# Short requests on GpSimd, another order of the head norms, zero products in waits, and a first feed-forward with rests

## The chip, the core and the metric

The kernel runs on one core of a Trainium2 chip. The core has TensorE (matrix products into PSUM), VectorE, ScalarE and GpSimd (elementwise work), SyncE (it issues most transfers), and 16 DMA engines that all issuing engines share. The metric is the device time of one execution in microseconds, lower being better. The engines run their own lists of instructions side by side and wait for each other through semaphores, so the order within a list is fixed by the program.

## The reference

Two transformer layers are applied to 256 tokens of width 1024, all in float32. Cut to what matters:

```python
# first block
sh1, sc1, gt1, sh2, sc2, gt2 = modulation(c, w_mod, b_mod)      # silu(c) @ w_mod + b_mod, for c and for c_ctx
hx = rms_norm(x, norm1_g) * (1 + sc1) + sh1                     # hc: the same of ctx
ax = latent_attention(qx, k_all, v_all)                         # q, k normalised by head, k_all: ctx and x
convx = short_conv(bx, cx, ux, conv_w)
x = x + gt1 * merge_out(ax, convx, attn_out_g, conv_out_g, w_out)  # norm by head of 64, then w_out
x = x + gt2 * hier_moe(hx2, w_group, w_router, w_gate, w_up, w_down)  # best group of 4, top 2 of its 8 experts
x = rms_norm(x, final_g)
# second block
ada = silu(c_2) @ w_ada + b_ada                                 # nine vectors of 1024
x = x + 0.5 * g1 * ((silu(h @ w_gate_half) * (h @ w_up_half)) @ w_out)   # ffn1, D_FF = 2816
x = x + g2 * ((sigmoid(gate_a) * mla(h) + sigmoid(gate_b) * chunk_attention(h, rel_bias)) @ w_out)
x = x + 0.5 * g3 * (ffn2, as ffn1)
return rmsnorm(x, final_norm)
```

## The kernel before, in words

Activations lie transposed, features on the 128 partitions in eight chunks (KD = 8) and the 256 tokens in the free dimension. Weights come by 2 MB tiles into a ring of six slots of one arena. Nothing is scheduled by a planner: each engine's program is written out by hand.

Most small and middle products are jobs (list `JOBS`). Job j writes PSUM bank j % 4. TensorE opens and closes it (`open_job`, `close_job`, semaphore `job_ready`), VectorE takes the result and frees the bank (`empty_job`, `job_emptied`). Both engines walk the list in one order, so a job that moves, moves on both.

**Head.** ScalarE issues the constants and the rows of gains and biases (`rows_a`, `rows_b`, turned to columns by TensorE), then the positions, the two router matrices and four blocks of the relative bias (L650 to L657). SyncE issues x, ctx and then the ring (L378). ScalarE computes SiLU of the conditions and the squares of x and ctx. TensorE multiplies the condition with w_mod as it arrives, four pieces `mod0` to `mod3` (L993). In TensorE's order the spreading of the token norms (L1013) and `bias_turn` (L1019) stand between mod1 and mod2. VectorE copies `bias_turn` (L1564), computes the angles of the rotary tables from the positions (L1570 to L1584), and only then copies the mod rows (L1594), from which the first norm's gain and shift come. The first large product is `z_k` (a call of `product`, L918), on the normalised ctx and w_kv.

**End of the first attention.** The last two of the eight attention steps put values after turned probabilities (L1114, L1126). The norms of the merged vector need the sum of squares in each head. `head_sums` (L1076) makes them by products of two columns, ScalarE takes the root (L754), VectorE the reciprocal (L1681), TensorE spreads it over the partitions (L1143), VectorE scales (L1687). `late_turn` brings the late part of the modulation into columns (L1002), and the four merge jobs follow.

**Router.** A norm (L934, L698, L1511, L1517, L711), the logits (L918 on `router`), h turned back to rows (L1163), some 6 us of short VectorE instructions that choose experts, the places of tokens (L918 on `route`), clearing of four banks with zeros (L1175), and `gather_pair` (L1183). Then the expert loop: 32 experts, two weight buffers, each with gate and up (L1217) and down (L1236).

**Feed-forward.** The hidden width 2816 is taken in 22 steps of 128. For gate and up both sides are split in a rounded high part and a rest, both of type fp32r, and three products are summed (L1291): ScalarE rounds (L818), VectorE subtracts (L1853). Steps 3 to 22 run in a loop of five turns with four steps each. ffn2 does the same for down (ScalarE L824 and L836, VectorE L1860 and L1899, three groups of eight products). ffn1 multiplies down in plain float32 (eight products in 16 passes). In ffn1 VectorE has beside it two items of w_ada per turn: eight multiply-adds each (L1474, L1477, `mod_item`), summed over partitions by four column products (`ada_columns`, L1323) and taken at L1923.

## Time and profile before

| | |
|---|---|
| median of 3 runs | 1641.79 us (1640.38 to 1643.27) |
| profiled execution | 1641.19 us, span 1639.4 us |
| mean granted clock of TensorE | 0.969 of 2.4 GHz |
| busy in the span | PE 1531.0, PEld 1072.7, DVE 519.7, ACT 331.5, POOL 23.7 us |
| chain that ended last | PE 71%, DMA 21%, DVE 4%, ACT's queue 2% |

PE is TensorE's products, PEld its weight loads, DVE VectorE, ACT ScalarE, POOL GpSimd. A letter q behind a name means the engine's queue, where it issues transfers. The busy time of TensorE is nearly the whole span, but a busy TensorE is not one at its peak, and a stage is read by what it waits for. The granted clock is 1.00 (2.4 GHz) or 0.50 (1.2 GHz) at any moment; values between are means over a stretch.

### The profile page before, as it was taken

The numbers are of one execution on the slowest core, as the hardware profiler recorded it, in microseconds if no ns is written. First come the engines' busy times: TensorE is split into PE (matmuls) and PEld (weight loads), VectorE is DVE, ScalarE is ACT, GpSimd is POOL, SyncE is SP. The second block draws the span as 40 slices with busy tenths as digits, with TensorE's granted clock in tenths as the row PEclk, the third lists the DMA queues.
The fourth block names the chain that finished last, engine by engine and source line by source line (L and its number), as shares of the span: only waits on it lengthen the run. The fifth ranks groups of instructions, "written<-read, shape, count | busy, mean of one in ns | idle before, by whom it ended". The sixth has DMA issues, their size and how long they took to land.

```text
span 1639.4 us, 22374 instructions
## 1 busy us (share of the span) xinstructions
PE 1531.0 (93%) x9594; PEld 1072.7 (65%) x9598; DVE 519.7 (32%) x926; ACT 331.5 (20%) x535; POOL 23.7 (1%) x31
## 2 busy tenths in 40 slices
PE   3899989999999999999999789999899989899996
PEld 1685864444444444434444479999787767799996
DVE  2446241111111111000111165555444362455553
ACT  1213231111111101111111132222110040343441
POOL 0003000000000000000000000000100000000000
PEclk8999879999999999999999989999999999999998
DMA  9648829999999999999999958878585222155540
GB/s 365 254 155 295 305 119 381 426 429 429 431 425 430 429 433 428 429 430 429 426 430 431 350 205 287 277 258 279 176 316 186 97 109 88 67 162 197 179 154 26
DMA packets 115290, 480.35 MB, mean 293 GB/s; under 512 B 6316, under 2 KB 53673, under 8 KB 95793
## 3 DMA queue, kind: packets, MB, share of 16 engines
q1 hardware_dynamic: 111680, 476.99, 74.0%
q10 hardware_dynamic: 3121, 1.18, 0.3%
q0 software_dynamic: 448, 1.59, 0.3%
q8 instruction: 31, 0.51, 0.1%
q14 instruction: 10, 0.08, 0.0%
HBM read 478.68 MB, written 1.06 MB: 293 GB/s over the span
## 4 chain that ended last, share of the span: by engine, by line
PE 71%; DMA 21%; DVE 4%; ACTq 2%; ACT 1%; issue 1%; DVEq 0%
DMA arena<-in_w_up_dram 21%; PE psum L918 17%; PE psum L1291 16%; PE psum L1217 12%; PE psum L1312 8%; PE psum L1236 5%; PE psum L1201 2%; PE psum L1183 2%; PE psum L934 1%; ACTq L657 1%; PE psum L1047 1%; PE psum L1097 1%; PE psum L1126 1%; PE psum L1114 1%; DVE rstd L1511 1%
## 5 line engine op out<-in xcount | busy, mean ns | idle before, releaser
L1217 PE MATMUL psum<-arena,squares 128*64 128x384 f32 x2048 | 341.4, 491 | 20.0 <-DMA arena<-in_w_up_dram 14.4
L1217 PEld LDWEIGHTS psum<-arena,squares 128*64 128x64 f32 x2048 | 146.7, 138 | 216.6 <-issue 183.2
L1808 DVE TENSOR_TENSOR mixT<-mixT,psum 128x384 f32<-128x384 f32 x32 | 26.5, 827 | 494.3 <-PE psum L1217 494.3
L918 PE MATMUL psum<-hT,arena 128*128 128x256 f32 (+1 forms) x784 | 173.1, 382 | 5.1 <-ACT hT L711 3.6
L1236 PE MATMUL psum<-arena,small 128*64 128x512 f32 x768 | 171.9, 596 | 0.0
L918 PEld LDWEIGHTS psum<-hT,arena 128*128 128x128 f32 (+1 forms) x784 | 149.2, 191 | 28.4 <-issue 5.7
L1291 PE MATMUL psum<-ff_x_hi,ff_w_hi 128*128 128x256 f32 x704 | 107.4, 295 | 8.8 <-ACT ff_x_hi L711 8.8
L1236 PEld LDWEIGHTS psum<-arena,small 128*64 128x64 f32 x768 | 52.3, 137 | 96.0 <-issue 94.1
L1853 DVE TENSOR_TENSOR ff_w_lo<-arena,ff_w_hi 128x2048 fp32r<-128x2048 f32 x44 | 100.8, 2290 | 16.4 <-ACT ff_w_hi L818 15.4
L1291 PEld LDWEIGHTS psum<-ff_x_hi,ff_w_hi 128*128 128x128 f32 x704 | 94.9, 194 | 12.4 <-issue 9.5
L1291 PE MATMUL psum<-ff_x_hi,ff_w_lo 128*128 128x256 f32 x704 | 100.4, 286 | 0.0
L1291 PE MATMUL psum<-ff_x_lo,ff_w_hi 128*128 128x256 f32 x704 | 100.0, 285 | 0.0
L1291 PEld LDWEIGHTS psum<-ff_x_hi,ff_w_lo 128*128 128x128 f32 x704 | 92.5, 195 | 0.0
L1291 PEld LDWEIGHTS psum<-ff_x_lo,ff_w_hi 128*128 128x128 f32 x704 | 92.1, 194 | 0.0
L818 ACT ACTIVATE ff_w_hi<-arena 128x2048 fp32r<-128x2048 f32 x44 | 83.6, 1900 | 0.1
L1312 PE MATMUL psum<-small,arena 128*128 128x256 f32 x352 | 80.3, 381 | 0.0
L1201 PE MATMUL psum<-small 64*128 64x256 f32 x528 | 74.6, 402 | 3.1 <-issue 3.1
L1477 DVE SCALAR_TENSOR_TENSOR mod_acc<-arena,cond,mod_acc 128x512 f32<-128x512 f32 x98 | 73.7, 752 | 3.5
L1312 PEld LDWEIGHTS psum<-small,arena 128*128 128x128 f32 x352 | 65.3, 190 | 8.0
L830 ACT ACTIVATE small<-psum 128x256 f32<-128x256 f32 x44 | 16.9, 384 | 254.5 <-PE psum L1291 254.5
L1201 PEld LDWEIGHTS psum<-small 64*128 64x128 f32 x528 | 45.5, 186 | 31.4 <-issue 28.4
L1183 PE MATMUL psum<-mixT,h_rows 128*128 128x128 f32 x544 | 65.6, 280 | 0.0
(282 smaller groups left out, 1369.4 us busy)
## 6 DMA issues: line engine op xcount, KB each, us to landing
arena<-in_w_gate_dram SPq DMA_DIRECT2D x32, 3072.0 KB, 33.5
arena<-in_w_up_dram SPq DMA_DIRECT2D x32, 3072.0 KB, 35.8
arena<-in_w_down_dram SPq DMA_DIRECT2D x32, 3072.0 KB, 32.0
arena<-in_ffn_w_in_dram SPq DMA_DIRECT2D x44, 1024.0 KB, 7.5
arena<-in_w_ada_dram SPq DMA_DIRECT2D x18, 2048.0 KB, 12.3
arena<-in_w_mod_dram SPq DMA_DIRECT2D x12, 2048.0 KB, 14.8
arena<-in_w_in_dram SPq DMA_DIRECT2D x11, 2048.0 KB, 13.8
arena<-in_ffn_w_out_dram SPq DMA_DIRECT2D x22, 1024.0 KB, 4.9
```

The lines of the kernel that those rows point to most:

```text
L818: nc.scalar.activation(ff_half(ff_w_hi[slot], half), ff_half(ring(slot), half), ACT.Copy)\
L830: nc.scalar.activation(silu_g[:, parity, :], bank[4 + parity][:, 0:T], ACT.Silu)\
L918: last = pe.matmul(dst, lhsT=lhs[i], rhs=rhs[i], start=(i == 0), stop=(i == n - 1))
L1183: last = pe.matmul(b[:, k * P:(k + 1) * P], lhsT=h_rows[:, tb, (4 * part + k) * P:(4 * part + k + 1) * P], rhs=pick[:, tb, :], start=(tb = ...
L1201: pe.matmul(bank[m // 2][:, (m % 2) * T:(m % 2 + 1) * T], lhsT=y_e[64 * half:64 * half + 64, c * P:(c + 1) * P], rhs=pick_wT[64 * half:64 ...
L1217: last = pe.matmul(b[64 * half:64 * half + 64, 0:HALF_E], lhsT=xeT[:, k, u * SLOTS:(u + 1) * SLOTS], rhs=w[:, k, half * HALF_E:(half + 1) ...
L1236: last = pe.matmul(bank[6][64 * half:64 * half + 64, :], lhsT=hiddenT[:, f % 3, 64 * (f // 3):64 * (f // 3) + 64], rhs=down[:, f, half * 5 ...
L1291: last = pe.matmul(bank[4 + parity][:, g * T:(g + 1) * T], lhsT=w[:, k, g, :], rhs=(ff_x_hi if x == "ready" else ff_x_lo)[:, k, :], start= ...
L1312: last = pe.matmul(bank[m // 2][:, (m % 2) * T:(m % 2 + 1) * T], lhsT=w[slot][:, half * D + m * P:half * D + (m + 1) * P], rhs=x[:, parity ...
L1477: i = nc.vector.scalar_tensor_tensor(out=mod_acc[:, u, :], in0=w[:, k, :], scalar=scalars[k], in1=mod_acc[:, u, :], op0=ALU.mult, op1=ALU.add)
L1808: nc.vector.tensor_tensor(hidden.rearrange("q (c p) -> q p c", c=3), gate_act.rearrange("q (p c) -> q p c", c=3), bank[5][:, 0:HALF_E].rea ...
L1853: nc.vector.tensor_tensor(ff_half(ff_w_lo[slot], half), ff_half(ring(slot), half), ff_half(ff_w_hi[slot], half), ALU.subtract).then_inc(se ...
```

## The change

Four edits:

1. The positions, the relative bias and the two router matrices are issued by GpSimd instead of ScalarE. The first two stand at the head of GpSimd's list, the router's behind the store of the turned bias. The job `rows_b` goes from the second place in the list to behind the eight turns of x and ctx.
2. At the end of the first attention the sums of squares of six chunks go behind the last values, `late_turn` goes behind the spread, and on VectorE two memsets for the experts go ahead of the merge.
3. `keep_busy(n)` multiplies n tiles of zeros (bfloat16, 512 columns) into bank 2, whose content isn't read. It stands at five places with 2, 5, 14, 14 and 14 products.
4. ffn1 multiplies down as ffn2 does, with high parts and rests. VectorE's two items of a turn are cut into single multiply-adds, spread over the steps by 5, 5, 5 and 1, and the column products go from steps j = 1 and 3 to j = 2 and 3.

```diff
+            pool.dma_start(turns[64:96, :], ins["positions_2"][0].partition_broadcast(32)).then_inc(sem("positions_loaded"), 16)
+            for b in range(4):
+                pool.dma_start(rel_bias_rows[:, b, :], ins["rel_bias_2"][0][385 - P * b:513 - P * b, :])\
+                    .then_inc(sem("rel_bias_loaded"), 16)
             pool.wait_ge(sem("job_emptied"), JOB["bias_turn"] + 1)
             pool.dma_start(bias_scratch, bias_rows).then_inc(sem("bias_stored"), 16)
+            pool.dma_start(router[:, :, 0:4], ...)      # and router[:, :, 4:36]
...
-            def feed_forward(key, split_out):
+            def feed_forward(key):
...
+            def keep_busy(n):
+
+                for _ in range(n):
+                    pe.matmul(bank[2][:, :], lhsT=zeros[:, 0:P], rhs=zeros[:, :], start=True, stop=True, skip_group_check=True)
...
-                    if key == "at1" and i == n + 2:
-                        head_sums((4, 5, 6, 7, 0, 1), 1)
...
             attention("at1")
+            head_sums((4, 5, 6, 7, 0, 1), 1)
             head_sums((2,), 2)
+            keep_busy(2)
             head_sums((3,), 3).then_inc(sem("mg_sums"), 1)
-            turn_pieces("late_turn", 2)
+            keep_busy(5)
             pe.wait_ge(sem("mg_rstd"), 1)
...
             sum_job("sum_n2", "n2", squares)
+            keep_busy(14)
...
+            keep_busy(14)
             b = open_job("positions")
...
+            keep_busy(14)
             pe.wait_ge(sem("job_emptied"), done_jobs[0])
...
+                def mod_steps(it, lo, hi):
+
+                    for n in range(lo, hi):
+                        u, j = n // 8, n % 8
...
                 with dve.Fori(0, FF_LOOPS) as it:
                     for j in range(4):
                         ff_rest(key, it * 4 + j + 3, 2 * (j // 2), j % 2)
+                        if with_ada and j == 3:
+                            mod_steps(it, 15, 16)
                         act(it * 4 + j + 2, (j + 1) % 2)
-                        if split_out:
-                            act_rest(it * 4 + j + 2, (j + 1) % 2)
-                            ff_out_rest(key, it * 4 + j + 3, 2 * (j // 2) + 1, j % 2)
...
+                        act_rest(it * 4 + j + 2, (j + 1) % 2)
+                        ff_out_rest(key, it * 4 + j + 3, 2 * (j // 2) + 1, j % 2)
+                        if with_ada:
+                            if j < 3:
+                                mod_steps(it, 5 * j, 5 * j + 5)
+                            if j >= 2:
+                                take_columns(it, j - 2)
```

The start of ScalarE's list before, up to its first computing instructions:

```order
L640 DMA consts<-in_shape_constants_dram 128x1704
L642 DMA rows_a<-in_vectors_a_dram 90x128
L643 DMA rows_a<-in_vectors_a_dram 16x128
L646 DMA rows_a<-in_vectors_a_dram 4x64 x2
L649 DMA rows_b<-in_vectors_b_dram 115x128
L650 DMA small<-in_positions_dram 32x256
L651 DMA router<-in_w_group_dram 128x8x4
L653 DMA router<-in_w_router_dram 128x8x32
L657 DMA rel_bias_rows<-in_rel_bias_dram 128x8 x4
L636 ACT_TABLE_LOAD
L636 ACTIVATE warmed<-consts 1x1 [waits consts_loaded]
```

On GpSimd's list now, from its start to the convolution:

```order
L572 UNCONDITIONAL_BRANCH [waits barrier_Pool_Activation_PE_DVE_SP_gather]
L584 DMA small<-in_positions_dram 32x256
L586 DMA rel_bias_rows<-in_rel_bias_dram 128x8 x4
L589 DMA bias_scratch<-small 8x512 [waits job_emptied]
L590 DMA router<-in_w_group_dram 128x8x4
L592 DMA router<-in_w_router_dram 128x8x32
L599 ISA
L599 TENSOR_SCALAR arena<-arena,cols_a 128x256 [waits job_emptied]
```

The four requests between rows_b and the table load are gone from ScalarE and stand on GpSimd, those of the router behind a wait for `bias_turn`.

TensorE at the end of the first attention, before (L1126 values, L1076 head sums, L1002 late_turn, L1143 spread):

```order
L1076 MATMUL psum<-consts,h_rows 128x2 [waits mg_squares]
L1076 MATMUL psum<-consts,h_rows 128x2 x11
L1126 MATMUL psum<-squares,arena 64x128 [waits second_back,first_back]
L1126 MATMUL psum<-squares,arena 64x128 x7
L1076 MATMUL psum<-consts,h_rows 128x2 [waits mg_squares]
L1076 MATMUL psum<-consts,h_rows 128x2
L1076 MATMUL psum<-consts,h_rows 128x2 [waits mg_squares]
L1076 MATMUL psum<-consts,h_rows 128x2
L1002 MATMUL psum<-block_select,mod_acc 128x8 [waits rows_copied,job_emptied]
L1002 MATMUL psum<-block_select,mod_acc 128x8 x3
L1143 MATMUL psum<-consts,head_rstd 64x128 [waits mg_rstd]
L1143 MATMUL psum<-consts,head_rstd 64x128 x31
```

The same place now (L1130, L1082, L1008 and L1149 are the same four lines, L918 is `keep_busy`):

```order
L1130 MATMUL psum<-squares,arena 64x128 [waits second_back,first_back]
L1130 MATMUL psum<-squares,arena 64x128 x7
L1082 MATMUL psum<-consts,h_rows 128x2 [waits mg_squares]
L1082 MATMUL psum<-consts,h_rows 128x2 x11
L1082 MATMUL psum<-consts,h_rows 128x2 [waits mg_squares]
L1082 MATMUL psum<-consts,h_rows 128x2
L918 MATMUL psum<-zeros 128x512 x2
L1082 MATMUL psum<-consts,h_rows 128x2 [waits mg_squares]
L1082 MATMUL psum<-consts,h_rows 128x2
L918 MATMUL psum<-zeros 128x512 x5
L1149 MATMUL psum<-consts,head_rstd 64x128 [waits mg_rstd]
L1149 MATMUL psum<-consts,head_rstd 64x128 x31
```

The first twelve sums moved behind the values, and seven zero products stand where late_turn stood.

VectorE in the last step (j = 3) of a turn of ffn1, before (L1853 rest of gate and up, L1893 act, L1923 take of the columns):

```order
L1853 TENSOR_TENSOR ff_w_lo_50<-arena,ff_w_hi_52 128x16x128
L1893 TENSOR_TENSOR small<-small,psum 128x256
L1921 REGISTER_ALU
L1923 ISA
L1923 TENSOR_TENSOR ada<-psum,cols_b 128x4
```

The same step now (L1915 a multiply-add, L1901 rest of the act, L1864 rest of the down weights):

```order
L1857 TENSOR_TENSOR ff_w_lo_50<-arena,ff_w_hi_52 128x16x128
L1914 REGISTER_ALU
L1915 SCALAR_TENSOR_TENSOR mod_acc<-arena,cond,mod_acc 128x512
L1895 TENSOR_TENSOR small<-small,psum 128x256
L1901 TENSOR_TENSOR ff_act_lo<-small,ff_act_hi 128x256
L1864 TENSOR_TENSOR ff_out_lo_54<-arena,ff_out_hi_56 128x1024
L1921 REGISTER_ALU
L1923 ISA
L1923 TENSOR_TENSOR ada<-psum,cols_b 128x4
```

Two rests and the sixteenth multiply-add came in; steps j = 0 to 2 have the two rests and five multiply-adds each.

## Rows read from the trace of the kernel before

**Rows 1.** Chain in order of time: start us, us, what.
```profile
517.53 35.87 DMA arena<-in_w_up_dram
...
602.83 38.50 DMA arena<-in_w_up_dram
```

**Rows 2.** Timeline of SyncE: start us, us, engine, line, operation.
```profile
249.21 0.36 SPq L419 DMA_DIRECT2D arena<-in_w_gate_dram  x1
```

**Rows 3.** Timeline of the head, with idle time before and releaser.
```profile
13.02 17.75 ACTq L657 DMA_DIRECT2D rel_bias_rows<-in_rel_bias_dram  x4
...
30.80 1.28 ACT L636 ACT_TABLE_LOAD   x1 [30.80 <-issue]
...
32.66 5.56 PE L993 MATMUL psum<-arena,cond 128*32 128x512 f32 x32 [11.35 <-ACT cond_late L666]
...
41.72 0.68 DVE L1564 COPY small<-psum 8x512 f32<-8x512 f32 x1 [1.18 <-PE psum L1019]
...
49.10 0.69 DVE L1594 COPY mod_acc<-psum 128x512 f32<-128x512 f32 x1
...
53.43 2.90 PE L918 MATMUL psum<-mixT,arena 128*128 128x256 f32 x6 [1.92 <-ACT mixT L711]
```

**Rows 4.** DMA landings by issue window (1.6, 3.7, 4.6 us on): count, KB, us.
```profile
arena<-in_w_mod_dram SPq DMA_DIRECT2D x1, 2048.0 KB, 15.1
...
arena<-in_w_mod_dram SPq DMA_DIRECT2D x1, 2048.0 KB, 28.6
...
q10 hardware_dynamic: 3057, 0.75, 6.6%
```

**Rows 5.** GpSimd's request: timeline, and its landing.
```profile
42.70 0.69 POOL L585 DMA_DIRECT2D bias_scratch<-small  x1 [42.24 <-DVE small L1564]
...
bias_scratch<-small POOLq DMA_DIRECT2D x1, 16.0 KB, 5.7
```

**Rows 6.** Timeline of the head norms; then one microsecond's busy times, clock, DMA.
```profile
169.91 2.84 PE L1076 MATMUL psum<-consts,h_rows 128*128 128x2 f32 x24
...
176.12 1.85 PE L1002 MATMUL psum<-block_select,mod_acc 128*128 128x8 f32 x8
...
177.90 6.36 PE L1143 MATMUL psum<-consts,head_rstd 128*64 128x128 f32 x64
...
174.00:175.00 1.00, 1.00 (x8) 0.79 (x4) 0.68 (x2) 0.22 (x1) 0.00 (x0) 0.50 1.16 215
```

**Rows 7.** Timeline of the router on TensorE, and zeros behind the experts.
```profile
219.14 6.81 PE L918 MATMUL psum<-router,hT 128*128 128x36 f32 x32 [3.60 <-ACT hT L711]
...
232.05 2.31 PE L918 MATMUL psum<-route,consts 128*128 128x32 f32 x10 [2.64 <-DVE route L1753]
...
235.73 1.49 PE L1175 MATMUL psum<-zeros 128*128 128x512 bf16 x3 [1.37 <-DVE picked L1774]
...
237.01 5.86 PE L1183 MATMUL psum<-mixT,h_rows 128*128 128x128 f32 x32
...
927.65 0.81 PE L1264 MATMUL psum<-zeros 128*128 128x512 bf16 x3 [0.16 <-issue]
```

**Rows 8.** Chain in order of time in ffn1 and, last row, in ffn2.
```profile
1043.31 3.46 PE psum L1312 x16
1046.76 5.74 PE psum L1291 x48
1053.29 3.56 PE psum L1312 x16
...
1438.50 2.83 PE psum L1312 x24
```

**Rows 9.** Timeline of VectorE, two rows in ffn1, two in ffn2.
```profile
1053.86 2.29 DVE L1853 TENSOR_TENSOR ff_w_lo<-arena,ff_w_hi 128x2048 fp32r<-128x2048 f32 x1 [0.24 <-issue]
...
1056.92 5.48 DVE L1477 SCALAR_TENSOR_TENSOR mod_acc<-arena,cond,mod_acc 128x512 f32<-128x512 f32 x7
...
1490.51 0.42 DVE L1893 TENSOR_TENSOR small<-small,psum 128x256 f32<-128x256 f32 x1 [2.64 <-ACT small L830]
...
1492.37 1.23 DVE L1860 TENSOR_TENSOR ff_out_lo<-arena,ff_out_hi 128x1024 fp32r<-128x1024 f32 x1 [0.52 <-ACT ff_out_hi L824]
```

More of the change, by code:

```diff
@@ L56 @@
 N_ROWS_B = 115
-JOBS = (["rows_a", "rows_b"] + [f"x_turn{i}" for i in range(4)] + [f"ctx_turn{i}" for i in range(4)]
+JOBS = (["rows_a"] + [f"x_turn{i}" for i in range(4)] + [f"ctx_turn{i}" for i in range(4)] + ["rows_b"]
         + ["spread_x", "spread_ctx", "bias_turn", "mod_turn", "z_k", "z_v", "z_q0", "z_q1", "z_gb0", "z_gb1"]
@@ L971, in linear_job, with turn_vectors @@
                 close_job(last)
+            pe.wait_ge(sem("zeros_ready"), 1)
             pe.wait_ge(sem("consts_loaded"), 16)
-            for name, rows, arrivals in (("rows_a", rows_a, 64), ("rows_b", rows_b, 16)):
+            def turn_vectors(name, rows, arrivals):
                 b = open_job(name)
```

120 lines of the change are left out of this document (55 added, 65 removed).

## The prediction, made before the changed kernel ran

> **What bounds the kernel now.** I read the page's chain of work first, then the chain in order of time, which splits the 1639.4 us of the span into three kinds of stretch. From 243 to 928 the expert loop runs. Its first experts are bound by TensorE, the later ones wait for their up matrices, some 36 to 38 us each [rows 1]. That stream of weights runs without a pause, and it starts when expert 0's gate product frees its buffer: the first reload goes out at 249.21 [rows 2]. So the loop's end is the time of its start plus a transfer that the change doesn't touch, and what is won ahead of the loop should come through whole. Behind the loop, the two feed-forward blocks and the middle are TensorE's. Ahead of it, from 0 to 53 us, TensorE mostly waits.
>
> The head's timeline shows for whom. ScalarE's first computing instruction starts at 30.80, because its queue is still issuing rel_bias loads from 13.02 on, stuck behind the element-wise router loads [rows 3]. SiLU of the condition comes out of that queue, so the first mod pieces, which TensorE multiplies at 32.66, wait for it, then the bias turn (copied at 41.72), the rope angles on VectorE, the copy of the mod rows at 49.10, and at 53.43 the first large product [rows 3].
>
> **Edit 1, requests to GpSimd and rows_b later.** ScalarE keeps six short issues, constants first (less than a megabyte), so its table load can start near 8. All that it did from there to the square root ended before the copy at 41.72, so it took less than 10.9 [rows 3], and now ends by 19, rows_b's later place included. What is late next is w_mod. Its first piece lands at 1.75 + 15.1 = 16.9, its fourth at 4.0 + 28.6 = 32.6, so they are 5.2 apart and the second comes at 22.1 [rows 4]. Some of the small packets that ran beside them (6.6% of 55 us, 3.7 us of each DMA engine, a part of it constants) now come later [rows 4]; I take 1 us off the second and 2.5 off the fourth: 21 and 30. Two pieces took 5.56 at the low clock, so one takes 1.9 to 2.8 [rows 3]; then spreads and bias turn, 3.0 (they took 41.72 less 38.22, 3.5, with 0.7 of waiting). The bias copy is at 21 + 2.4 + 3.0 = 26.4 to 27.5, the angles end 7.4 later at about 34.5 (49.10 less 41.72), behind the fourth piece's product (30 + 2.8) [rows 3], and the large product starts 11.7 after the bias copy (53.43 less 41.72): 39. w_kv, a megabyte right behind the fourth piece of two, lands half a spacing later, at about 33, so it isn't late. Gain 14.5. Everything behind is paced by TensorE and follows.
>
> GpSimd's own requests are the unknown price. Its one early request took 0.69 to issue and landed after 5.7, at a time when the DMA engines were full [rows 5]; five of them take 4 to 5 us to issue and should land by about 15 to 20, beside the big transfers. The need is at 24. The other bound is the slowest of rows 4, 28.6 us behind its issue: landing near 30 leaves a gain of 10. Upper end 16.5, where the pieces run at the full clock and all small packets are out of the way. I take 14.5, near the row of GpSimd itself. The router's two requests are needed only at 219 [rows 7], and GpSimd's convolution waits for the last projection, far behind them.
>
> The Trainium skill, page "SBUF — State Buffer", section "SBUF: two separate sides", speaks against this edit: a DMA issued from GpSimd has its descriptors written by GpSimd's cores, and VectorE locks them out while it runs an operation in a two-port mode. By that rule the requests at the start would be held by VectorE's memsets (the first things that it does) and cost a microsecond or two, and the router's would be held beside the angle chain, which costs nothing. The trace's own row agrees that little is lost: the store was issued in 0.69 us beside that chain [rows 5].
>
> **Edit 2, head norms.** Before, 24 two-column products ran at 169.91 for 2.84 us ahead of the last attention values, the clock fell to 1.2 GHz (0.50 at 174), and the spread at 177.90 took its 64 products in 6.36 at it [rows 6]. Now the values (1.1 at the full clock) go first, so VectorE's copy and ScalarE's square of chunk 3 hide behind those products; late_turn (1.85 at the low clock) goes from before the spread to behind it. Sums: 169.9 + 1.1 + 2.84 + 0.5 + two zero products + 0.5. ScalarE's root and the reciprocal take about 0.9, and five zero products run beside them. Zero products are 0.215 apart at 2.4 GHz and 0.43 at 1.2 GHz (three in 0.81 and in 1.49, one being 0.38 and 0.63) [rows 7]. With the full clock the spread starts at 176.4 and takes 3.6, late_turn 1.0: the merge starts at 181 instead of 184.2, gain 3. With the low clock: 178.6 + 6.4 + 1.9 = 186.9, loss 2.7. The clock fell before while TensorE was busy all the time, in narrow products, and these stay. I take +0.5.
>
> **Edit 3, zeros in the router's waits.** The waits are 3.60 before the logits, 2.64 before the positions and 1.37 before the bank clearing [rows 7]. 14 zero products take 3.0 at the full clock and 6.0 at the half. At the full clock throughout: the second half of the logits (6.81 in all) saves 2.3; from there the chain is VectorE's up to the clearing at 235.73, and the third batch ends about 0.9 behind it; clearing saves 0.6; the gather 237.01 (5.86) saves 2.9; the moved memsets give 0.2. Sum 5.1. At the half clock throughout: 2.4 + 3.4 + 4.6 = 10.4 lost. The logits' 36 columns are narrow too, so I expect the clock to fall again for a part of it: gain 3.5, bounds -10.4 and +5.1. The skill's page "TensorE: Matmul & The Clock Gate", section "Part 1: The HAM clock gate (the "warmup" mystery)", says that the clock follows how busy TensorE has recently been. By that the filled waits would hold it, +8.1 for edits 2 and 3 together, against my +4. Rows 6 don't agree that busy is all: it fell in a stretch with no idle time.
>
> **Edit 4, down products with rests.** A step of ffn1 is gate_up, 5.74, and down, 3.46 (16 passes), every other one with 0.79 of four column products (1053.29 less 1046.76 and 5.74). ffn2's down with rests takes 2.83 for 24 [rows 8]. 22 steps by 0.63 are 13.9, the upper end. VectorE gets 22 act rests (0.43) and 22 out rests (1.23) beside the 5.48 of multiply-adds for each of ten items. From the act at 1490.51 to the end of the out rest at 1493.60 is 3.1 with ScalarE's roundings between; then five multiply-adds at 5.48/7 = 0.78, 3.7 with a cheaper first one, and ff_rest 2.29 [rows 9]. That is 9.0 with the starts overlapping a little, against TensorE's 8.57. It slips 0.2 to 0.4 in each of two steps. At the two steps with columns it catches up, but there ff_rest waits for the columns' take and ends 0.57 + 2.29 = 2.86 after the down started [rows 8, 9], where down now gives only 2.83 of cover: 0 to 0.2 more. So a turn of four steps takes 36.7 instead of 38.6 (35.9 without stalls). ada_full5 is asked for one step earlier, two steps of 8.57 behind its request; a piece of the same size landed in 15.1 under the head's heavier load [rows 4], so it's hidden. 13.9 less 0.7 in each of four turns is 11.1; I take 11.5. Lower end 8: 0.3 more in each step that VectorE paces.
>
> **Sum.** 14.5 + 0.5 + 3.5 + 11.5 = 30.0. The profiled execution took 1641.19 (span 1639.4), 0.6 under the median of 1641.79. 1641.2 - 30 = 1611.2, and 0.3 to 0.6 for the median: 1611.5.
>
> **Rivals.**
> First, everything holds: clock at 2.4 GHz ahead of the experts (+8.1) and VectorE in step (+13.5), with a head of 15: 36.6, so 1605. For it: the waits shrink to almost none. Against: narrow products stay, and 9.0 is over 8.57. 15%.
> Second, VectorE paces ffn1: with semaphore waits between the cut multiply-adds a step costs 9.3 or more, and take and ff_rest follow each other. ffn1 gives 6: 1617. 12%.
> Third, the zeros don't lift the clock, or come when it is low: 14 in each wait at 0.43 lose 10.4, the head norm 2.7. Then 14.5 + 11.5 - 13 = 13: 1628. Against: a wait that was empty is now full of 512-column products. 10%.
> Fourth, the other side: the bias turn waits for GpSimd's requests. rel_bias stands ahead of the third and fourth mod piece on TensorE and ahead of the angles on VectorE, so every microsecond that it lands after 24 is paid. From 39 on the head gains nothing; from 54 on (24 + 30) the kernel is slower. At 60 the large product starts at 75, 21.6 later than before, and with 15.5 from the other edits the time is 1648. For it: one small packet at a time among full DMA engines. Against: the 5.7 of rows 5. 3% for slower, 5% for a partial loss (1620).
> The change doing nothing would need the head's 30.80 to stay, and the removed issues are its only content.
>
> **Chances.** Forecast 55% (its own range 1606 to 1616), first rival 15, second 12, third 10, fourth 8. The range 1602 to 1624 leaves out the third rival, the bad end of the fourth and a little at the lower end, 18 in 100. Within 0.2% (3.3 us, what a measurement tells apart) of before: 2%. Slower: 3%. Faster: 95%.
>
> **What would show it.** ScalarE's table load near 8 instead of 30.80, and the first large product near 39; GpSimd's requests landed before 24; the spread's and the gather's duration and the granted clock there; experts starting 18 to 19 earlier and the up waits unchanged; a turn of ffn1 of 36.7, with TensorE waiting on ff_w_lo. Wrong would make it: a wait of TensorE on rel_bias, zero products at 0.43 ending after what they cover, or turns over 37.5.

## The result, and the profile after

The changed kernel takes 1611.07 us (median of 4 runs, 1610.54 to 1613.65) against 1642.53 of the kernel before beside it: a ratio of 0.9817, 95% interval 0.9805 to 0.9828. The profiled execution took 1610.54 us, the least of the four, with a span of 1607.8. It is 31.6 us shorter than the span before. The forecast was 1611.5, by a sum of 30.0.

The page of the changed kernel, busy times and two of the DMA queues (packets, MB, share of 16 engines), and below them the same two queues on the page of before; q10 is ScalarE's, q0 GpSimd's:

```profile
PE 1520.5 (95%) x9817; PEld 1064.9 (66%) x9823; DVE 554.5 (34%) x970; ACT 361.6 (22%) x579; POOL 28.5 (2%) x38
...
q0 software_dynamic: 688, 1.79, 0.3%
q10 hardware_dynamic: 417, 0.99, 0.2%
```

```profile
q10 hardware_dynamic: 3121, 1.18, 0.3%
q0 software_dynamic: 448, 1.59, 0.3%
```

The moved requests were 2704 packets on ScalarE's queue (3121 less 417). On GpSimd's the same 0.2 MB are 240 packets (688 less 448).

**Head.** The timeline of the changed kernel, then the landing of one of GpSimd's four relative-bias requests:

```profile
1.29 0.70 POOL L584 DMA_DIRECT2D small<-in_positions_dram  x1 [0.84 <-POOLq L2112]
2.00 2.18 POOL L586 DMA_DIRECT2D rel_bias_rows<-in_rel_bias_dram  x4
3.70 1.28 ACT L644 ACT_TABLE_LOAD   x1 [3.70 <-issue]
...
22.17 3.57 PE L999 MATMUL psum<-arena,cond 128*32 128x512 f32 x16 [2.96 <-DMA arena<-in_w_mod_dram]
...
26.76 0.93 PE L1025 MATMUL psum<-consts,rel_bias_rows 128*8 128x128 f32 x7
...
27.84 0.68 DVE L1568 COPY small<-psum 8x512 f32<-8x512 f32 x1 [0.55 <-PE psum L1025]
...
32.99 3.28 PE L999 MATMUL psum<-arena,cond 128*32 128x512 f32 x16 [3.48 <-DMA arena<-in_w_mod_dram]
...
36.35 0.69 DVE L1598 COPY mod_acc<-psum 128x512 f32<-128x512 f32 x1 [1.23 <-PE psum L999]
...
40.13 2.47 PE L912 MATMUL psum<-mixT,arena 128*128 128x256 f32 x5 [1.92 <-ACT mixT L709]
...
rel_bias_rows<-in_rel_bias_dram POOLq DMA_DIRECT2D x1, 4.0 KB, 5.9
```

ScalarE's table load starts at 3.70 instead of 30.80 [rows 3]. The five requests on GpSimd are issued within 3 us and the last is there before 10, so nothing waits for them. What TensorE waits for now is w_mod: 2.96 ahead of the second piece, 3.48 ahead of the fourth. The fourth piece is on the chain that ended last; in order of time:

```profile
3.99 28.96 DMA arena<-in_w_mod_dram
...
32.99 3.33 PE psum L999 x16
```

The large product starts at 40.13 instead of 53.43 [rows 3].

**Head norms and router**, on TensorE:

```profile
158.67 3.29 PE L1082 MATMUL psum<-consts,h_rows 128*128 128x2 f32 x28
...
163.12 2.29 PE L918 MATMUL psum<-zeros 128*128 128x512 bf16 x5
165.35 3.76 PE L1149 MATMUL psum<-consts,head_rstd 128*64 128x128 f32 x64
...
201.33 2.97 PE L918 MATMUL psum<-zeros 128*128 128x512 bf16 x13
204.88 4.91 PE L912 MATMUL psum<-router,hT 128*128 128x36 f32 x32 [0.58 <-ACT hT L709]
...
213.28 2.97 PE L918 MATMUL psum<-zeros 128*128 128x512 bf16 x13 [0.22 <-issue]
...
221.01 3.73 PE L1192 MATMUL psum<-mixT,h_rows 128*128 128x128 f32 x32
```

The spread takes 3.76 instead of 6.36 [rows 6], the logits 4.91 instead of 6.81 and the gather 3.73 instead of 5.86 [rows 7]. The five zero products ahead of the spread took 2.29, 0.45 apart (1.2 GHz), and overran what they cover: VectorE's reciprocal was done at 163.97.

**The expert loop** starts at 225.52 instead of 243.64. The chain in order of time shows its waits as long as before [rows 1], and the loop takes 667.0 us in both traces, so the 18.1 us come through whole:

```profile
499.37 35.89 DMA arena<-in_w_up_dram
...
540.73 38.50 DMA arena<-in_w_up_dram
```

**ffn1**, one turn of four steps in the chain in order of time:

```profile
1026.76 0.79 PE psum L1326 x8
1027.55 2.93 PE psum L1315 x24
1030.48 0.07 issue
1030.55 6.01 PE psum L1300 x48
1036.56 2.83 PE psum L1315 x24
1039.38 5.84 PE psum L1300 x48
1045.22 2.83 PE psum L1315 x24
1048.05 5.77 PE psum L1300 x48
...
1057.54 5.76 PE psum L1300 x48
...
1064.09 2.93 PE psum L1315 x24
```

A down with rests takes 2.83 to 2.93 for 3.46 to 3.56 [rows 8]. From 1027.55 to 1064.09 a turn is 36.54. Where it loses time, a gate_up shows 6.01 or 5.84 instead of 5.76: stalls on ff_w_lo of 0.3 and 0.1.

**Between the experts and ffn1** nothing was changed, and yet the stretch went from 49.6 to 46.4 us. The forecast had no term for these 3.1 us; several of the experiments below bear on them.

### The profile page after: what moved, and what is told of

Read it like the earlier page. It is cut to its first block, busy times and chain, and to the rows that moved or that the text cites. A ratio compares the mean times of both kernels' runs of the same rounds, so it can differ in the third digit from the quotient of the medians.

```text
span 1607.8 us, 22925 instructions
## 1 busy us (share of the span) xinstructions
PE 1520.5 (95%) x9817; PEld 1064.9 (66%) x9823; DVE 554.5 (34%) x970; ACT 361.6 (22%) x579; POOL 28.5 (2%) x38
## 4 chain that ended last, share of the span: by engine, by line
PE 72%; DMA 23%; DVE 3%; ACT 1%; issue 1%; SPq 0%; DVEq 0%; ACTq 0%
DMA arena<-in_w_up_dram 21%; PE psum L912 17%; PE psum L1300 16%; PE psum L1226 12%; PE psum L1315 8%; PE psum L1245 5%; PE psum L1210 2%; DMA arena<-in_w_mod_dram 2%; PE psum L1192 2%; PE psum L933 1%; PE psum L1103 1%; PE psum L1053 1%; PE psum L1118 1%; PE psum L1130 1%; PE psum L999 1%; DVE rstd L1514 1%
## 5 line engine op out<-in xcount | busy, mean ns | idle before, releaser
L1226 PE MATMUL psum<-arena,squares 128*64 128x384 f32 x2048 | 341.4, 491 | 20.0 <-DMA arena<-in_w_up_dram 14.5
L1857 DVE TENSOR_TENSOR ff_w_lo<-arena,ff_w_hi 128x2048 fp32r<-128x2048 f32 x44 | 100.8, 2290 | 15.6 <-ACT ff_w_hi L816 14.6
L1210 PEld LDWEIGHTS psum<-small 64*128 64x128 f32 x528 | 45.6, 186 | 31.3 <-issue 28.4
L788 ACT ACTIVATE small<-psum 128x384 f32<-128x384 f32 x32 | 15.7, 490 | 218.5 <-PE psum L1234 218.5
L1192 PEld LDWEIGHTS psum<-mixT,h_rows 128*128 128x128 f32 x544 | 62.2, 192 | 0.1
L1864 DVE TENSOR_TENSOR ff_out_lo<-arena,ff_out_hi 128x1024 fp32r<-128x1024 f32 x44 | 54.0, 1226 | 22.0 <-ACT ff_out_hi L822 22.0
L793 ACT ACTIVATE small<-psum 128x512 f32<-128x512 f32 x32 | 19.1, 597 | 175.5 <-PE psum L1245 175.5
## 6 DMA issues: line engine op xcount, KB each, us to landing
arena<-in_w_mod_dram SPq DMA_DIRECT2D x12, 2048.0 KB, 14.2
```

The lines of the kernel that those rows point to most:

```text
L793: nc.scalar.activation(y_e, bank[6][:, :], ACT.Copy).then_inc(sem("y_ready"), 1)
L1192: last = pe.matmul(b[:, k * P:(k + 1) * P], lhsT=h_rows[:, tb, (4 * part + k) * P:(4 * part + k + 1) * P], rhs=pick[:, tb, :], start=(tb = ...
L1210: pe.matmul(bank[m // 2][:, (m % 2) * T:(m % 2 + 1) * T], lhsT=y_e[64 * half:64 * half + 64, c * P:(c + 1) * P], rhs=pick_wT[64 * half:64 ...
L1226: last = pe.matmul(b[64 * half:64 * half + 64, 0:HALF_E], lhsT=xeT[:, k, u * SLOTS:(u + 1) * SLOTS], rhs=w[:, k, half * HALF_E:(half + 1) ...
L1857: nc.vector.tensor_tensor(ff_half(ff_w_lo[slot], half), ff_half(ring(slot), half), ff_half(ff_w_hi[slot], half), ALU.subtract).then_inc(se ...
L1864: nc.vector.tensor_tensor(ff_out_lo[slot][:, part], ring(slot)[:, part], ff_out_hi[slot][:, part], ALU.subtract)\
```

## The experiments

The changed kernel, measured twice, gave medians of 1611.07 and 1613.20, and in the second measurement its executions lie 9.8 us apart (1610.57 to 1620.32, at mean granted clocks of 0.980 and 0.972). So the reading goes by stretches. Each row is one profile of one execution, which need not be a typical one. z_k is the start of the first large product; the columns behind it are the lengths from there to the first piece of the late modulation inside the attention, to the first merge, from the sum behind the merge to the first expert, of the expert loop up to the end of the last expert's gate and up products, from there to ffn1, of ffn1, and from its end to ffn2 (all from the start times of TensorE's rows, us). The merge (27.7 in all) and ffn2 (192.5 to 192.9) are left out.

| kernel | z_k | to late0 | to merge | router | experts | to ffn1 | ffn1 | to ffn2 |
|---|---|---|---|---|---|---|---|---|
| before | 53.4 | 77.4 | 53.4 | 31.7 | 667.0 | 49.6 | 216.0 | 247.5 |
| requests_only | 39.4 | 78.5 | 52.0 | 31.2 | 666.9 | 49.3 | 215.9 | 247.5 |
| ffn1_plain | 40.2 | 77.8 | 53.0 | 29.6 | 666.8 | 49.3 | 215.9 | 247.5 |
| no_zeros | 40.7 | 77.8 | 51.9 | 30.9 | 668.6 | 50.8 | 204.1 | 248.7 |
| norm_old | 38.5 | 77.1 | 53.3 | 27.9 | 667.2 | 49.4 | 204.1 | 248.8 |
| router_late | 40.5 | 78.6 | 51.3 | 27.9 | 667.6 | 49.4 | 204.1 | 248.8 |
| changed | 40.1 | 78.5 | 51.3 | 27.9 | 667.0 | 46.4 | 204.1 | 248.8 |
| after_again | 39.9 | 78.1 | 53.0 | 29.5 | 667.1 | 49.5 | 204.1 | 248.8 |
| items_whole | 40.3 | 78.6 | 51.3 | 27.9 | 667.1 | 46.4 | 217.2 | 245.4 |
| head_zeros | 39.1 | 75.6 | 53.0 | 30.8 | 667.4 | 50.6 | 204.0 | 248.7 |
| more_zeros | 38.7 | 75.6 | 52.9 | 29.6 | 668.5 | 53.0 | 203.1 | 244.3 |
| zeros_but_ffn1 | 39.4 | 75.6 | 51.3 | 27.8 | 667.6 | 49.3 | 204.1 | 245.7 |
| wide_between | 40.0 | 75.6 | 50.2 | 29.5 | 667.1 | 49.4 | 204.2 | 245.7 |
| wide_all | 39.2 | 75.6 | 53.3 | 29.5 | 667.0 | 45.9 | 202.4 | 244.2 |

Ratios below are to the kernel before on the same chip (its medians: 1641.62 beside requests_only, ffn1_plain, no_zeros and more_zeros; 1640.47 beside norm_old, head_zeros, router_late and zeros_but_ffn1; 1641.29 beside after_again, items_whole, wide_between and wide_all).

**requests_only.** The kernel before with the requests moved and nothing else:

```diff
-            act.dma_start(turns[64:96, :], ins["positions_2"]...)      # and two router, four rel_bias requests
+            pool.dma_start(turns[64:96, :], ins["positions_2"]...)     # and four rel_bias, at the head of GpSimd's list
+            pool.dma_start(router[:, :, 0:4], ...)                     # and router 4:36, behind the bias store
```

> The kernel before with one part of the change: positions, relative bias and router requests go out from GpSimd; rows_b keeps its second place among the jobs. Theory: ScalarE's blocked queue was the whole of edit 1, and rows_b's place is worth nothing, since TensorE waits for w_mod behind it: z_k starts near 40.1 as in the changed kernel and the first attention 12.2 earlier: 1642.5 - 12.2 = 1630.3 (1628.5 to 1631.5). Rival: TensorE waits for rows_b ahead of the eight turns, and that delays SiLU and the pieces: z_k at 41 to 42, 1632.

Measured: 1627.47 us, ratio 0.9919 (0.9902 to 0.9936), 14.2 less than before and 1.0 below the range that I gave. TensorE did wait for rows_b ahead of the eight turns, and its product started at 16.54:

```profile
16.54 0.45 PE L977 MATMUL psum<-consts,rows_b 115*128 115x115 f32 x1 [6.03 <-DMA rows_b<-in_vectors_b_dram]
```

The chain of this profile goes through that wait, and on over the turns, the pieces, the bias turn and the angles to the copy of the mod rows. The fourth piece isn't on it: its product started at 32.51, took 1.92 and was done before the angles.

```profile
3.31 13.19 DMA rows_b<-in_vectors_b_dram
...
35.65 0.70 DVE mod_acc L1592
```

So the theory is wrong in its reason: here it isn't w_mod that sets z_k. The rival's wait is real and on the path, but its price was too high: z_k starts at 39.4 and not at 41 to 42. The seven profiles with rows_b in its new place and no zero products in the head have z_k between 38.5 and 40.7. A gain from the move of rows_b isn't shown; it would be at most some 0.9 (39.4 less 38.5), within what the profiles differ by. The requests are all of edit 1 that can be seen.

**router_late.** In the changed kernel the two router requests are issued behind the convolution.

```diff
             pool.dma_start(bias_scratch, bias_rows).then_inc(sem("bias_stored"), 16)
-            pool.dma_start(router[:, :, 0:4], ...); pool.dma_start(router[:, :, 4:36], ...)
...
             nc.gpsimd.tensor_tensor(mixT[:, 4:8, :], conv_out, gate_b, ALU.mult).then_inc(sem("conv_done"), 1)
+            pool.dma_start(router[:, :, 0:4], ...); pool.dma_start(router[:, :, 4:36], ...)
```

> The changed kernel with the two router requests issued behind the convolution (near 132 instead of 29.3). Theory: the fourth piece of w_mod is set by the rate at which the 2 MB pieces come, one in 5.0 to 5.5 us, and the small packets took none of it: it lands at 32.9 as now, 1611 (1610 to 1612). Rival: the router's small packets, under way from 29.3 on, hold it up: it lands near 31.4, the large product starts up to 1.2 us earlier (the angles end at 35.1), 1609.9.

Measured: 1614.60, ratio 0.9844 (0.9829 to 0.9859). The fourth piece's product, on TensorE:

```profile
33.09 3.54 PE L999 MATMUL psum<-arena,cond 128*32 128x512 f32 x16 [3.60 <-DMA arena<-in_w_mod_dram]
```

It is at 33.09 against 32.99 with the router's packets beside it. Of the eight profiles without zero products in the head, where this product starts between 32.35 and 33.09, it is the latest: taking the router's packets away from beside the fourth piece gained nothing that can be seen. The median is outside of what I gave, above the 1613.20 of the changed kernel's second measurement too, but the stretches up to the experts are those of the changed kernel within 0.4 us each, the experts within 0.6; what is longer is the way to ffn1, 49.4 against 46.4.

**no_zeros.** The changed kernel without the 49 zero products:

```diff
-            keep_busy(2)        # between the head sums
-            keep_busy(5)        # ahead of the spread
-            keep_busy(14)       # ahead of logits, positions and bank clearing
```

> The changed kernel without its 49 zero products in waits (the new order of the head norms stays). Theory: they keep the granted clock up. Without them the clock falls to 1.2 GHz at the spread and from the logits to the gather again, as it did before the change: the stretch from the squares' sum to the first expert goes from 27.7 us back to about 31.5, the spread from 3.7 to about 6, less 1.4 us of overrun at the spread: 1616.5 (1614 to 1619). Rival: the zero products do nothing and the new order alone made the difference: then only the overrun of 1.4 goes, 1609.7.

Measured: 1617.35, ratio 0.9847 (0.9819 to 0.9874). Windows of the router in the changed kernel and in this one (us; length, busy time of PE, PEld, DVE, ACT and POOL with their counts, granted clock, DMA share, GB/s):

```profile
197.66:225.52 27.86, 26.46 (x154) 19.64 (x154) 16.01 (x78) 12.00 (x25) 0.00 (x0) 0.94 0.29 114
```

```profile
198.11:229.00 30.89, 22.18 (x113) 20.18 (x112) 16.02 (x78) 11.96 (x25) 0.00 (x0) 0.72 0.26 103
```

TensorE has 41 products more in the first and is through 3.0 us sooner: the clock is 0.94 instead of 0.72. The medians alone would not show it: this interval overlaps those of both measurements of the changed kernel (0.9805 to 0.9828 and 0.9811 to 0.9854). The stretch does: 30.9 to 31.7 in the three profiles without zero products there, 27.8 to 30.8 in the eleven with them. At the attention's end no gain is to be seen: 51.9 without zero products, 51.3 in four profiles with them and 53.0 in four others.

**norm_old.** The changed kernel with the head norms as before, the router's zero products kept:

```diff
+                    if key == "at1" and i == n + 2:
+                        head_sums((4, 5, 6, 7, 0, 1), 1)
...
-            head_sums((4, 5, 6, 7, 0, 1), 1)
             head_sums((2,), 2)
-            keep_busy(2)
             head_sums((3,), 3).then_inc(sem("mg_sums"), 1)
-            keep_busy(5)
+            turn_pieces("late_turn", 2)
```

On VectorE late_turn goes back ahead of the scaling.

> The changed kernel with edit 2 undone: the first 24 two-column products ahead of the last values, late_turn ahead of the spread, no zero products there; the router's stay. Theory: edit 2 is worth about nothing, since the kernel with GpSimd's requests alone started its merge at 169.9 as the changed kernel did, after a large product that started 0.7 earlier: 1611 (1609.5 to 1613). Rival: the changed kernel's own trace is right, where 14.1 us at the merge stand against 12.2 ahead of the head sums: undone it costs 1.9, 1613.

Measured: 1615.63, ratio 0.9854 (0.9838 to 0.9869). That is above the numbers of both theories and 2.4 above after_again, with overlapping intervals; the profile fell on the least of the four executions, 1611.84. The stretch is 53.3. The old order gives 53.4, 52.0 and 53.3 (mean 52.9) in three profiles, the new one with its zero products 51.3 four times and 53.0 four times (mean 52.1; wide_between and wide_all have another set). By these means edit 2 is worth 0.8, between the two theories. That isn't clear of the spread, since single profiles of one program differ by 1.7 there; the 1.9 came from a comparison of one profile with one.

**ffn1_plain.** The changed kernel with the first feed-forward of before, with its order of multiply-adds (in short, in `down` for ffn1):

```diff
-                    parts = ((ff_out_hi, ff_act_hi), (ff_out_lo, ff_act_hi), (ff_out_hi, ff_act_lo))
+                        parts = (({slot: ring(slot)[:, 0:2 * D]}, ff_act),)
```

> The changed kernel with the first feed-forward as before (down in plain float32, multiply-adds of an item together). Theory: edit 4 is worth what the loop shows, 214.4 against 202.6 us: 1611.1 + 11.8 = 1622.9 (1621 to 1624.5). Rival: a part of these 11.8 is given back behind the loop, since low-clock stretches behind it fall differently: 1621.3, with the middle 1.5 us shorter than in the changed kernel.

Measured: 1622.53 (1616.66 to 1629.69), ratio 0.9884 (0.9845 to 0.9924). ffn1 is 215.9 against 204.1, so 11.8. The rival has its point as well: the way to ffn2 is 247.5 in the three profiles with the old ffn1 and 248.7 or 248.8 in six with the new one (items_whole apart, with 245.4). 1.3 is given back there.

**items_whole.** The changed kernel with the eight multiply-adds of an item together:

```diff
-                        if with_ada and j == 3:
-                            mod_steps(it, 15, 16)
...
-                            if j < 3:
-                                mod_steps(it, 5 * j, 5 * j + 5)
+                            if j % 2 == 0:
+                                mod_steps(it, 4 * j, 4 * j + 8)
```

> The changed kernel with each w_ada item's eight multiply-adds together again, behind the first and the third step of a turn, and down still with rests. Theory: ff_rest of the next step comes 8 x 0.78 behind the out rest; VectorE's two steps of 11.4 and 5.3 fit into TensorE's 17.1 in sum, but its lead is under one step, so TensorE waits some 2.3 us in two steps of every turn: a turn of 41.2 instead of 36.5, 1611 + 23 = 1634 (1628 to 1638), all of edit 4's gain and more gone. Rival: the two steps even each other out, and cutting the items was not needed: 1611 to 1613.

Measured: 1627.79, ratio 0.9924 (0.9903 to 0.9944). Timelines of VectorE and of TensorE in this kernel:

```profile
1037.31 5.47 DVE L1915 SCALAR_TENSOR_TENSOR mod_acc<-arena,cond,mod_acc 128x512 f32<-128x512 f32 x7
1042.70 2.29 DVE L1857 TENSOR_TENSOR ff_w_lo<-arena,ff_w_hi 128x2048 fp32r<-128x2048 f32 x1
```

```profile
1045.04 1.22 PE L1300 MATMUL psum<-ff_x_hi,ff_w_hi 128*128 128x256 f32 x8 [2.17 <-DVE ff_w_lo L1857]
...
1064.71 1.13 PE L1300 MATMUL psum<-ff_x_hi,ff_w_hi 128*128 128x256 f32 x8
```

The theory's stall is there at the expected size, 2.17, but once in a turn. The item of the third step is caught up in the fourth, since there is no item in it and VectorE anyway waits for the columns; its gate_up at 1064.71 stands without a wait. ffn1 takes 217.2, 13.0 more than the changed kernel, where I gave 23; stalls of 2.2 in four turns and of 0.4 in the first make 9.1. Part of the rest is the clock: in the chain the gate_up behind the stall takes 7.52 in the turn shown and 6.02 in the next. The median is 14.6 above that of after_again, just below the range that I gave. Without the cut the rests would have brought next to nothing: ffn1 and the way to ffn2 are 462.6 together, against 463.5 before and 452.9 in the changed kernel.

**head_zeros.** Zero products in the head's four waits (the second argument of `keep_busy` is the bank):

```diff
                 piece(f"mod{i}", bank[4], cond, i == 0, False)
+                if i == 0:
+                    keep_busy(12, 6)
...
                 piece(f"mod{i}", bank[4], cond, False, i == 3)
+                keep_busy(14 if i == 2 else 3, 6)
             turn_pieces("mod_turn", 1)
+            keep_busy(8, 6)
```

> The changed kernel with zero products in four waits of the head alone: 12 behind mod0, 14 behind mod2, 3 behind mod3, 8 behind mod_turn. Theory: the clock then stays at 2.4 GHz from z_k on, z_k starts about 1 us sooner and the head sums at 154.3 instead of 158.7, and that comes through but for what the low clock ahead of the spread and the router takes back: 3 of 4.4 us, 1608 (1606.5 to 1610). Rival: a low-clock stretch that is avoided here comes back at the next narrow products, as where the zero products at all places gained 1.0 by the first expert: 1610.

Measured: 1610.23, ratio 0.9810 (0.9794 to 0.9826). From z_k to late0 it takes 75.6, in this and in the four others with these zero products, against 77.1 to 78.6 in the seven of the changed kernel's family without: 1.5 to 3.0 is gained. z_k itself, which was to start 1 us sooner, starts at 38.7 to 40.0 in these five, against 38.5 to 40.7. In this profile the gain is lost again by the first expert (226.22 against 225.52): the spread and the router fell into a low clock. The rival describes this profile, which fell on the slowest of the four executions (1614.65), and the median too is the rival's 1610; the theory's range ended there.

**more_zeros and zeros_but_ffn1.** The first adds zero products at ten places, the head's four as above and six more; the second leaves out the two between the experts and ffn1:

```diff
+            keep_busy(14, 4)                    # behind the experts; only more_zeros
...
             sum_job("sum_ffn1", "ffn1", squares)
+            keep_busy(15, 4)                    # only more_zeros
...
                 last.then_inc(sem(f"{key}_sum_done"), 1)
+                keep_busy(14, 4)                # both: behind each feed-forward
...
             sum_job("sum_mix", "mix", squares)
+            keep_busy(15, 4)                    # both: and behind sum_ffn2
```

> The changed kernel with zero products in eight more waits of TensorE: 12, 14, 3 and 8 in the head (behind mod0, mod2, mod3 and mod_turn), 14 behind the experts, 15 between the norm's sum and the first product of ffn1, of the middle and of ffn2, 14 behind each feed-forward. Theory: these waits bring the low-clock stretches that follow them (10.2 us behind 42.8 in the clock's record, 3.4 and 6.8 at ffn1's start, 3.4 and 6.8 at the middle's, 3.4 and 6.8 ahead of ffn2; each costs half of its length). All of them gone is 20; overruns and what stays take a part: 12 us faster, 1599 (1595 to 1604). Rival: the zero products come when the clock is low already, take 0.43 each and overrun their waits: 1613 to 1616.

> The changed kernel with zero products in the head's four waits, behind both feed-forwards and ahead of the middle and ffn2, but none between the experts and ffn1, where the version with all of them took 53.0 us instead of 46.4. Theory: the zero products between the experts and ffn1 brought nothing, or harm; without them that stretch takes 46.4 to 49.5, the head gives 3, behind ffn1 1.7, in the middle 2.8: 1603.5 (1601 to 1606). Rival: those 53.0 were one execution's own clock and not the zero products: then leaving them out gains nothing over 1606.0.

Measured: 1606.01, ratio 0.9770 (0.9741 to 0.9799), and 1604.50, ratio 0.9777 (0.9749 to 0.9804). The two can't be told apart; the first is outside of its range, the second inside. Behind ffn1 the way to ffn2 is 244.3 and 245.7, and 244.2 and 245.7 in wide_all and wide_between, against 248.7 or 248.8 in six profiles. But items_whole has 245.4 without a zero product in these waits, so a shift of the low-clock stretches alone can give as much. Of the 20 us that I had counted for all low stretches, and the 12 that I took, 5 to 7 came. Between the experts and ffn1 the clock was lower with the zero products than without, in the one profile there is.

**wide_between and wide_all.** Both start from zeros_but_ffn1. The first has

```diff
                                          rhs=K("heads64").rearrange("p (h n) -> p h n", h=2)[:, :, 0], start=True, stop=True)
+                    if len(chunks) > 1:
+                        keep_busy(1)
...
-            keep_busy(5)
+            keep_busy(3)
```

and the second, on top, between the experts and ffn1:

```diff
+            keep_busy(14, 4)                    # behind the experts
...
+                if i == 2:
+                    keep_busy(7, 4)             # ahead of col_ada1, which waits 1.7 us
...
                     last = pe.matmul(b[:, 2 * m:2 * m + 2], lhsT=mod_acc[:, u, m * P:(m + 1) * P], rhs=K("select"),
+                    if m % 2 == 1:
+                        keep_busy(1, 4)         # in every ada column job
...
+            keep_busy(15, 4)                    # behind sum_ffn1
```

> The version with zero products in the head, behind the feed-forwards and ahead of the middle and ffn2; now also one wide zero product behind each four of the first 24 two-column products of the head sums (six, 1.3 us), and three instead of five ahead of the spread. Theory: the low clock at the spread, which came in every profile so far, with the 512-column zero products in the waits or without, comes from the two-column products themselves; with wide products between them the clock stays at 2.4 GHz, late0 to merge takes 51.2 (51.3 to 52.95 before), and the median is 1603 (1601 to 1605.5). Rival: the low stretch comes all the same, the six products only cost: 54, and 1606.

> The same and, between the experts and ffn1, zero products in the three waits (14, 7 and 15) and one behind every second two-column product of the ada columns (1.7 us in all). Theory: the low stretches there come from those narrow products too; the stretch takes 47 instead of 49.3 to 53, 1601.5 (1598 to 1604). Rival: they come anyway, as where only the waits were filled (53.0): the products cost 1.7 and the overruns: 1606 to 1608.

Measured: 1605.14, ratio 0.9773 (0.9757 to 0.9788), and 1601.52, ratio 0.9751 (0.9732 to 0.9769). At the head sums the two profiles disagree. In wide_between the clock held (window from the sums to the merge):

```profile
155.66:165.84 10.18, 10.01 (x116) 8.98 (x116) 4.78 (x11) 1.25 (x5) 0.00 (x0) 1.00 0.75 169
```

In wide_all, with the same instructions there, it fell, and the spread took 5.29:

```profile
162.04 5.29 PE L1157 MATMUL psum<-consts,head_rstd 128*64 128x128 f32 x64
```

So for the head sums neither theory is shown. Between the experts and ffn1 wide_all has the shortest of all these stretches, 45.9, where wide_between has 49.4 and the changed kernel's first profile 46.4. Its window, and below it that of the changed kernel run again:

```profile
892.41:938.27 45.86, 41.97 (x266) 24.29 (x270) 18.00 (x33) 12.23 (x19) 0.00 (x0) 1.00 0.95 332
```

```profile
895.22:944.71 49.49, 37.70 (x225) 21.49 (x226) 18.00 (x33) 12.21 (x19) 0.00 (x0) 0.90 0.90 315
```

TensorE does 4.3 us more in it and ends 3.6 us sooner, at a granted clock of 1.00. wide_all has the lowest median of all: 1601.52 against 1613.20 of the changed kernel beside it on the same chip, with intervals that don't touch. How much of it is due to the wide products between the narrow ones stays open: wide_between and more_zeros, with 1605.14 and 1606.01, have intervals that overlap with its own.

**after_again.** The changed kernel itself:

> The changed kernel once more, beside the other kernels of this group. Its stretches in the other profiles differ only where the clock's low stretches fall, so its 1611.1 should come out between 1611 and 1615. Theory: its first profile had a short way from the experts to ffn1 by luck of the clock (46.4 us, where seven other profiles took 49.3 to 53.0); most executions take 49.3, so the median is nearer 1613. Rival: 46.4 belongs to this program, the profile repeats it, and the median stays at 1611.1.

Measured: 1613.20 (1610.57 to 1620.32), ratio 0.9833 (0.9811 to 0.9854). The way to ffn1 is 49.5. All in all 46.4 came in 2 of the 10 profiles that have the program of the changed kernel in this stretch, 49.3 to 49.5 in six and 50.6 to 50.8 in two. The ten profiles bear the theory out; the two medians alone do not, since their intervals overlap.

## Why the prediction came out right

The time was right to 0.4 us in the first measurement and to 1.7 in the second. By the runs the parts are these:

| part | predicted | by the runs |
|---|---|---|
| edit 1 | 14.5 | 14.2 (its requests alone: 1627.47 against 1641.62) |
| edit 2 | 0.5 | 0.8 (means of the stretch to the merge, not clear of their spread) |
| edit 3 | 3.5 | 2.4 (means of the router stretch: 31.3 without, 28.9 with zero products) |
| edit 4 | 11.5 | 11.8 in ffn1, 1.3 given back behind it |
| not in the sum | 0 | 3.1 between the experts and ffn1 in the first profile, none in the second |

The parts make 27.9. The second measurement shows 28.1; the first shows 31.5, and 27.9 and 3.1 are 31.0. So the first match with 30.0 was in part luck: edits 1 and 3 came out smaller than predicted, part of edit 4 was given back, and the clock in one execution made up for it.

Edit 1, step by step. ScalarE's table load came at 3.70 instead of near 8, and ScalarE was ready by 19.5 (I had 19). The fourth piece of w_mod was to land 2.5 us sooner, at 30, since small packets would be out of its way; it landed at 32.95, and before it had landed at 32.6. This step failed. The share of DMA time of small packets [rows 4] wasn't time that the large transfer lost: router_late took more of them away, and the piece came no sooner. What came of the late landing hung on the clock. The piece's product took 3.28 in the changed kernel, at granted clocks of 0.59 and 0.56 from 32 to 34 and from 34 to 36. So the mod rows were copied at 36.35 instead of behind the angles (35.1, expected 34.5), and z_k came at 40.1 instead of 39. In norm_old, with the same head, the piece came no sooner, but its product ran at the full clock:

```profile
32.76 1.92 PE L999 MATMUL psum<-arena,cond 128*32 128x512 f32 x16 [3.20 <-DMA arena<-in_w_mod_dram]
```

There the copy was at 34.75 and z_k at 38.5. With 1.92 the changed kernel's product too would have ended before its angles. By z_k, edit 1 gained 13.3 in the changed kernel's profile and 14.0 in requests_only. The unknown price, GpSimd's requests, was lower than I had it: 2.9 us to issue and 5.7 to 6.3 to land where I took 4 to 5 and a landing by 15 to 20. The Trainium skill says, on its page "SBUF — State Buffer", section "SBUF: two separate sides", that VectorE keeps GpSimd from writing descriptors while it runs an instruction in a two-port mode. The requests went out at 1.29 and 2.00, while VectorE set buffers to zero until 2.6, and took 0.55 to 0.70 each; this trace shows no loss of the microsecond or two that I had worked out from it. Whether these memsets run in such a mode isn't shown.

Edits 2 and 3. That the clock would hold for a part was right, and so was the middle course between 2.4 GHz throughout and nothing. What I hadn't seen is how the part comes about: the router takes 27.9 in five profiles, 29.5 in five and 30.8 in one, with the same zero products. By the Trainium skill's page "TensorE: Matmul & The Clock Gate", section "Part 1: The HAM clock gate (the "warmup" mystery)", which says that the clock follows how busy TensorE has recently been, the two edits were to bring 8.1; they brought 3.2. norm_old shows a window that speaks against the busy share being all, as rows 6 did, ten microseconds with TensorE busy for 9.98 and the clock at 0.56:

```profile
159.00:169.00 10.00, 9.98 (x85) 9.42 (x81) 4.21 (x11) 0.70 (x2) 0.00 (x0) 0.56 0.53 121
```

TensorE had not been idle since 150.59 either. It ran 24 two-column products, then from 157.42 values of 128 columns, and in these the clock fell (1.00 in the microsecond up to 157, then 0.76 and 0.50):

```profile
154.65 2.84 PE L1082 MATMUL psum<-consts,h_rows 128*128 128x2 f32 x24
```

```profile
157.00:158.00 1.00, 1.00 (x11) 0.98 (x12) 0.00 (x0) 0.00 (x0) 0.00 (x0) 0.76 1.01 199
158.00:159.00 1.00, 1.00 (x14) 0.94 (x10) 0.00 (x0) 0.00 (x0) 0.00 (x0) 0.50 1.01 168
```

That the narrow products are the cause isn't shown: the clock fell at this place in wide_all too, with a wide product behind each four of them.

Edit 4. The turn was to take 36.7 and took 36.54, with TensorE waiting for ff_w_lo in the step behind the columns, as the working said. A step of VectorE without columns takes 8.6 to 8.7 where I had 9.0, so it slips by less than 0.2 instead of 0.2 to 0.4. The rival of a pacing VectorE is real in another order of the multiply-adds: items_whole.

What was missing is a term for the clock behind the edits: the way from the experts to ffn1 changes between 46.4 and 50.8 us without a changed instruction.

The rival of the other side, a bias turn that waits for GpSimd, had nothing to it: the requests were there 17 us ahead of the need.

## What to carry to other kernels

Look at what the engine that is needed first has in its queue: here 26 us of issuing small requests stood ahead of ScalarE's first instruction, and moving them to an engine with nothing to do was worth 14 us, nearly half of the change. Before a gain is counted for a transfer, ask whether the transfer in question is held up by those removed or runs at its own rate. And where the clock falls in some executions, compare stretches over several profiles of like kernels, not one profile with one: a stretch that nobody touched moved by 3.1 us here, as much as a whole edit was worth.

## What the runs showed of the hardware

- On ScalarE's queue before, the larger router request took 8.24 us to issue and the relative bias behind it 17.75 [rows 3], 16.28 of it for the first of the four. GpSimd issues the two router requests in 1.01 and 0.89, and they land after 7.3 and 7.4 instead of 28.6 and 32.4. All the moved requests are 240 packets there instead of 2704. Before, and then now:

```profile
4.75 8.24 ACTq L653 DMA_DIRECT2D router<-in_w_router_dram  x1
```

```profile
29.33 1.01 POOL L590 DMA_DIRECT2D router<-in_w_group_dram  x1
30.33 0.89 POOL L592 DMA_DIRECT2D router<-in_w_router_dram  x1
```

- The first and the fourth 2 MB piece of w_mod landed at 16.9 and 32.6 before and at 17.2 and 32.95 in the changed kernel, 5.2 to 5.3 us a piece, though 2704 packets of small requests had been taken off ScalarE's queue.
- The granted clock fell to 1.2 GHz while TensorE was busy without a pause, behind 24 two-column products (0.76 in the microsecond from 157, 0.50 in the next, in norm_old). With 512-column zero products in the waits and between the narrow ones it stayed at 2.4 GHz over the 45.9 us ahead of ffn1 in the one profile there is. At the head sums the same measure held in one profile and not in the other; why stays open.
- The expert loop took 666.8 to 667.6 us in twelve profiles, and 668.5 and 668.6 in two in which the last expert's products took 7.08 instead of 5.38; the waits for the up matrices in the chain were 35.9 and 38.5 us long before and after.
